# Restaging the mLSTM heads of a two-layer streaming encoder: outputs by token, broadcasts by DMA, tails behind the next head

## The reference, cut to what matters

```python
dlog = b[l] - b[s] + i[s]                      # b: running sum of log forget gates; causal
m_t  = max(a[l], max_s dlog);  a = b + m
w    = exp(dlog - m_t);  w_in = exp(a - m_t)
qk   = (q k^T) * w
num  = qk @ v + w_in * (q @ C)
den  = sum_s qk + w_in * (q @ n)
hc   = num / max(|den|, exp(-m_t))
C    = w_in_last * C + (w_last * k)^T v ;  n = w_in_last * n + (w_last * k)^T 1
out  = sigmoid(o_pre) * head_norm(hc) * gain   # mean and variance over the head's 128 features
y    = concat(gla, out) @ c_w_out
```

## Time and profile before

| | |
|---|---|
| median of 3 runs | 1608.72 us |
| profiled execution, its own time | 1611.44 us |
| its span | 1609.8 us |
| PE, weight loads of PE | 92%, 86% busy |
| VectorE, ScalarE, GpSimd | 45%, 32%, 5% busy |
| mean granted TensorE clock | 0.946 of full |
| chain that ended last | PE 81%, VectorE 8%, ScalarE 4% |

### The profile page before, as it was taken

The page is one execution under the profiler, slowest core; times in us unless marked ns, Lnnn a source line. Parts: engine busy times, 40 slices in busy tenths (PEclk is TensorE's granted clock), DMA queues, the critical chain, the costliest instruction groups (busy, mean ns, idle before and its releaser), DMA issues.

```text
span 1609.8 us, 29103 instructions
## 1 busy us (share of the span) xinstructions
PE 1474.7 (92%) x11188; PEld 1380.6 (86%) x11188; DVE 722.2 (45%) x1167; ACT 522.1 (32%) x792; POOL 85.5 (5%) x99
## 2 busy tenths in 40 slices
PE   5889999989999999999698988888969999999997
PEld 3878888979999999998587867666969999999997
DVE  4664565463333333335734354444563333333344
ACT  4344344242222222223533343332242212222233
POOL 0000000001100110110100000000001100110110
PEclk9899999999999999999797977887989999999999
DMA  9445253763352344223021111110213323323322
GB/s 327 114 146 166 89 161 108 268 244 115 91 183 79 91 142 132 79 70 77 5 77 32 52 36 37 36 36 17 79 54 90 90 81 90 91 81 89 92 66 82
DMA packets 223377, 160.78 MB, mean 100 GB/s; under 512 B 9226, under 2 KB 209628, under 8 KB 223196
## 3 DMA queue, kind: packets, MB, share of 16 engines
q1 hardware_dynamic: 211728, 117.18, 25.0%
q10 hardware_dynamic: 6764, 25.30, 4.2%
q0 software_dynamic: 4832, 17.58, 3.5%
HBM read 156.46 MB, written 3.57 MB: 99 GB/s over the span
## 4 chain that ended last, share of the span: by engine, by line
PE 81%; DVE 8%; ACT 4%; issue 3%; DMA 2%; ACTq 1%; DVEq 0%; SPq 0%
PE ring L535 68%; PE core_j L451 2%; DVE weight_low L413 1%; PE core_j L751 1%; ACT weight_high L408 1%; PE core_k L756 1%; PE core_k L451 1%; PE core_k L1156 1%; DMA weight_raw<-in_a_w_out 1%; PE core_k L1198 1%; DMA mixer_area<-in_w_mod 1%; PE core_k L1115 1%; PE core_k L1118 1%; ACTq L1907 1%; PE ring L1175 0%
## 5 line engine op out<-in xcount | busy, mean ns | idle before, releaser
L535 PE MATMUL ring<-normed_high,weight_high 128*128 128x272 f32 x2128 | 455.9, 296 | 31.1 <-DVE normed_low L633 14.0
L535 PE MATMUL ring<-normed_high,weight_low 128*128 128x272 f32 x2128 | 447.9, 292 | 0.0
L535 PE MATMUL ring<-normed_low,weight_high 128*128 128x272 f32 x2128 | 447.8, 293 | 0.0
L535 PEld LDWEIGHTS ring<-normed_high,weight_high 128*128 128x128 f32 x2128 | 343.0, 193 | 41.9 <-issue 36.5
L535 PEld LDWEIGHTS ring<-normed_low,weight_high 128*128 128x128 f32 x2128 | 343.5, 194 | 0.0
L535 PEld LDWEIGHTS ring<-normed_high,weight_low 128*128 128x128 f32 x2128 | 340.9, 193 | 0.0
L413 DVE TENSOR_TENSOR weight_low<-weight_raw,weight_high 128x1024 fp32r<-128x1024 f32 x197 | 261.1, 1327 | 136.9 <-ACT weight_high L408 134.8
L408 ACT ACTIVATE weight_high<-weight_raw 128x1024 fp32r<-128x1024 f32 x197 | 206.7, 1050 | 168.4 <-PE ring L535 142.1
L535 PE MATMUL ring<-mixed_high,weight_high 128*128 128x272 f32 x960 | 203.1, 293 | 11.5 <-DVE weight_low L413 9.1
L535 PE MATMUL ring<-mixed_high,weight_low 128*128 128x272 f32 x960 | 200.9, 291 | 0.0
L535 PE MATMUL ring<-mixed_low,weight_high 128*128 128x272 f32 x960 | 200.6, 291 | 0.0
(11 more groups left out here) (378 smaller groups left out, 1150.0 us busy)
## 6 DMA issues: line engine op xcount, KB each, us to landing
weight_raw<-in_w_ffn_in SPq DMA_DIRECT2D x88, 512.0 KB, 3.9
mixer_area<-in_w_mod ACTq DMA_DIRECT2D x12, 2048.0 KB, 10.7
mod_weight<-in_w_mod POOLq DMA_DIRECT2D x16, 1024.0 KB, 5.9
weight_raw<-in_w_ffn_out SPq DMA_DIRECT2D x32, 512.0 KB, 3.7
weight_raw<-in_a_w_in SPq DMA_DIRECT2D x24, 512.0 KB, 4.9
weight_raw<-in_c_w_in SPq DMA_DIRECT2D x20, 512.0 KB, 3.9
mixer_area<-in_w_mod SPq DMA_DIRECT2D x7, 1024.0 KB, 13.3
weight_raw<-in_w_ffn_out SPq DMA_DIRECT2D x16, 384.0 KB, 3.3
```

Source lines behind the costliest of these rows:

```text
L535: last = pe.matmul(PS[p.slot][:, half, 0:HALF], w[n.slot][:, k, :], x[:, k, half * HALF:(half + 1) * HALF], start=(k == 0 and w is WH and ...
```

## The change

1. Row broadcasts by DMA. The two spreads of RA and RI go; SyncE issues a DMA that reads one partition's row (544 floats, 2176 bytes) 128 times and writes it to all partitions: `BA[h % 2]` for the decay row, `WB[h % 2]` for w_in. Both are double-buffered. VectorE reads BA from SBUF for the exponents.
2. The spread of exp(-m) goes. It is transposed once, in the GLA stage, into a small tile FLOOR (tokens on partitions, one column for each head).
3. The heads' outputs are made by token: tokens on partitions, 128 features and the denominator as column 129 (VO has one ones column, states are 129 wide): one chain of matmuls in place of two.
4. Statistics by `bn_stats` and `bn_aggr` on VectorE, the reciprocal root by an integer start value and three Newton steps on a tile of 128 x 5; then one pass for each block that subtracts the mean and scales, transposes back by PE (`head_transposes`), gate (`gated_out`), high and low halves with the gain folded in.
5. The order: the heads are written out. The tail of head h-1 stands between the steps of head h on all three engines. The next head's projection is cut in two halves around the update (`project_part`); in the last head its place is taken by parts of the output projection's first two chains (`out_part`). Head 0's o_pre projection stands in the tail of the last GLA head, in halves around the variance. The output projection uses ahead=2.

```diff
-                sp.wait_ge(s_nd, h)
+                sp.wait_ge(s_mkt, h)
                 sp.dma_start(WQK, t["mlstm_w_qk"][0, h]).then_inc(s_mw2, 16)
                 sp.dma_start(WV, t["mlstm_w_v"][0, h]).then_inc(s_mw2, 16)
-                sp.dma_start(SEL[0:HEADS, :], t["selectors"][h]).then_inc(s_mw2, 16)
+                sp.wait_ge(s_rexp, 2)
+                if h >= 2:
+                    sp.wait_ge(s_ex, h - 1)
+                sp.dma_start(BA[h % 2], RA[h:h + 1, :].unsqueeze(1).to_broadcast([1, P, T])).then_inc(s_ba, 16)
+                if h >= 2:
+                    sp.wait_ge(s_cn, h - 1)
+                sp.dma_start(WB[h % 2], RI[h:h + 1, :].unsqueeze(1).to_broadcast([1, P, T])).then_inc(s_bw, 16)
+                sp.wait_ge(s_nd, h)
...
                 head_mean(pe, OT, s_o, 2 * i + HEADS + 1)
+                if i:
+                    item_part(7, range(0, KD // 2))
                 head_var(pe, OSQ, s_osq, 2 * i + HEADS + 1)
+                if i:
+                    item_part(7, range(KD // 2, KD))
...
+                def next_part(first):
+                    if last:
+                        out_part(*((0, 1) if first else (2, 3)))
+                    else:
+                        project_part(pe, Turn(W_ML, 2, 2, h), r(h, 4), range(0, 4) if first else range(4, KD))
...
+                next_part(True)
+                pe.wait_ge(s_kw, h + 1)
+                for b in range(NB + 1):
+                    n = P if b < NB else TS
+                    mm = pe.matmul(J[:, b // 3, (b % 3) * (P + 1):(b % 3 + 1) * (P + 1)], KW[0:n, b, :], VO[0:n, b, :],
+                                   start=True, stop=True)
+                mm.then_inc(s_cu, 1)
+                next_part(False)
                 pe.wait_ge(s_am, h + 1)
-                spread(RF, K).then_inc(s_be, 1)
-                pe.wait_ge(s_kw, h + 1)
-                pe.wait_ge(s_enb, h + 1)
-                for b in range(NB):
-                    pe.matmul(K[:, b // 2, (b % 2) * 256:(b % 2) * 256 + 256], KW[:, b, :], VO[:, b, :],
-                              start=True, stop=True)
-                pe.matmul(J[:, 1, 0:256], KW[0:TS, NB, :], VO[0:TS, NB, :], start=True, stop=True).then_inc(s_cu, 1)
-                if not last:
-                    project(pe, Turn(W_ML, 2, 2, h), r(4))
+                pe.wait_ge(s_qi, h + 1)
                 pe.wait_ge(s_cn, h + 1)
-                pe.wait_ge(s_qi, h + 1)
-                for b in range(NB):
-                    cols = slice(b * P, (b + 1) * P)
-                    for part, dst in ((0, K), (1, J)):
-                        c = slice(part * P, (part + 1) * P)
-                        pe.matmul(dst[:, 0, cols], VO[:, b, c], AM[:, b, :], start=True, stop=(b == 0))
-                        if b:
-                            pe.matmul(dst[:, 0, cols], CN[:, b - 1, c], QI[:, cols], start=False, stop=True)
-                for part, dst in ((0, K[:, 1, P:P + TS]), (1, J[:, 1, 0:TS])):
-                    c = slice(part * P, (part + 1) * P)
-                    pe.matmul(dst, VO[0:TS, NB, c], AM[0:TS, NB, 0:TS], start=True, stop=False)
-                    mm = pe.matmul(dst, CN0[:, c], QI[:, TP:T], start=False, stop=True)
+                for b in range(NB + 1):
+                    n, cols = (P, slice(b * P, (b + 1) * P)) if b < NB else (TS, slice(TP, T))
+                    mm = pe.matmul(by_block(K, b), AM[0:n, b, 0:n], VO[0:n, b, :], start=True, stop=(b == 0))
+                    if b:
+                        mm = pe.matmul(by_block(K, b), QI[:, cols], CN[:, b - 1, :] if b < NB else CN0,
+                                       start=False, stop=True)
                 mm.then_inc(s_nd, 1)
-                pe.wait_ge(s_dabs, h + 1)
-                head_mean(pe, OT, s_o, h + 2 * HEADS)
-                head_var(pe, OSQ, s_osq, h + 2 * HEADS)
-            with pe.Fori(0, HEADS - 1) as h:
-                head(h)
-            head(HEADS - 1, True)
+            out_part(4, 5)
+            head_transposes(HEADS - 1)
+            out_part(6, 7)
...
+            def moments(h):
+                dve.wait_ge(s_nd, h + 1)
+                dve.wait_ge(s_d2, h + 1)
+                for b in range(NB + 1):
+                    n = P if b < NB else TS
+                    st.add(dve.bn_stats(BN6[0:n, b, :], by_block(K, b, P)))
+                st.wait()
+                for b in range(NB + 1):
+                    n = P if b < NB else TS
+                    st.add(dve.bn_aggr(MV[0:n, b, :], BN6[0:n, b, :]))
+                st.done(dve.tensor_tensor(DEN2, DEN2, FLOOR[:, :, h], ALU.max))
+                st.done(dve.tensor_tensor(VAR, MV[:, :, 1], DEN2, ALU.add))
+            def scale(h):
+                rsqrt(dve, st, VAR, RSTD, RTMP)
+                for b in range(NB + 1):
+                    n = P if b < NB else TS
+                    ins = dve.tensor_scalar(ON[0:n, b, :], by_block(K, b, P), MV[0:n, b, 0:1], RSTD[0:n, b:b + 1],
+                                            ALU.subtract, ALU.mult)
+                    if b < NB:
+                        st.add(ins)
+                ins.then_inc(s_on, 1)
+            def gated_out(h):
+                dve.wait_ge(s_otr, h + 1)
+                dve.wait_ge(s_gah, h + KD + HEADS + DONE0)
+                g = TG[h % 2]
+                st.add(dve.scalar_tensor_tensor(out=OB[:, 0:TP], in0=g[:, 0:TP], scalar=1.0, in1=K[:, 0, :],
+                                                op0=ALU.add, op1=ALU.mult))
+                dve.scalar_tensor_tensor(out=OB[:, TP:T], in0=g[:, TP:T], scalar=1.0, in1=K[:, 1, 0:TS],
+                                         op0=ALU.add, op1=ALU.mult).then_inc(s_ob, 1)
+            def low(h):
+                dve.wait_ge(s_ob, h + 2 * HEADS + 1)
+                st.wait()
+                dve.wait_ge(s_gah, h + KD + HEADS + DONE0 + 1)
+                dve.scalar_tensor_tensor(out=GL[:, h + 4, :], in0=OB, scalar=HGAIN[:, h + 8:h + 9],
+                                         in1=GH[:, h + 4, :].bitcast(F32), op0=ALU.mult,
+                                         op1=ALU.subtract).then_inc(s_glo, 1)
...
+                if h:
+                    low(h - 1)
+                if last:
+                    lo_of(dve, w(h, 3))
+                else:
+                    exponents(h + 1)
...
+        def rsqrt(dve, st, v, y, tmp):
+            st.done(dve.tensor_scalar(y.bitcast(I32), v.bitcast(I32), 1, None, ALU.logical_shift_right))
+            st.done(dve.tensor_scalar(y.bitcast(I32), y.bitcast(I32), -1.0, float(0x5f3759df), ALU.mult, ALU.add))
+            for _ in range(3):
+                st.done(dve.tensor_tensor(tmp, y, v, ALU.mult))
+                st.done(dve.scalar_tensor_tensor(out=tmp, in0=tmp, scalar=-0.5, in1=y, op0=ALU.mult, op1=ALU.mult))
+                st.done(dve.scalar_tensor_tensor(out=y, in0=tmp, scalar=1.5, in1=y, op0=ALU.add, op1=ALU.mult))
...
-            out_act(act, W_OUT1, R_OUT1, 3)
-            hi_of(act, Turn(W_FFN1 + 1))
+            out_act(act, W_OUT1, R_OUT1, 3, ahead=2)
```

More of the change, by code:

```diff
@@ L23 @@
 U32 = mybir.dt.uint32
+I32 = mybir.dt.int32
 ACT = mybir.ActivationFunctionType
@@ L516, in project, with project_part @@
             last.then_inc(s_used, 1)
+        def project_part(pe, n, p, ks):
+            if ks[0] == 0:
+                pe.wait_ge(s_lo, n.index + 2)
+                pe.wait_ge(s_free[p.slot], p.before)
+            for k in ks:
+                last = product(pe, n, p, k, KD, (HNH, HNL))
+            if ks[-1] == KD - 1:
+                last.then_inc(s_used, 1)
         def project_two(pe, n, p, normed):
@@ L705, in transpose_blocks, with out_two, out_pe @@
             return pe.transpose(dst_s, src[:, TP:T], IDENT)
[L707 to L713, removed]
-                for j in range(2):
-                    last = product(pe, Turn(w, j), Turn(p, j), k, len(order), (GH, GL))
+        def out_two(pe, w, p, order, s_tiles, tiles, part=None):
+            part = range(len(order)) if part is None else part
+            if part[0] == 0:
+                for j in range(2):
+                    pe.wait_ge(s_lo, w + j + 2)
+                    pe.wait_ge(s_free[Turn(p, j).slot], Turn(p, j).before)
+            for n in part:
+                pe.wait_ge(s_tiles, tiles - (len(order) - 1 - n))
+                for j in range(2):
+                    last = product(pe, Turn(w, j), Turn(p, j), order[n], len(order), (GH, GL))
                     if n == len(order) - 1:
                         last.then_inc(s_used, 1)
-        def out_pe(pe, w, p, kt, s_tiles, tiles, order=None):
-            if order is not None:
+        def out_pe(pe, w, p, kt, s_tiles, tiles, order=None, begun=False):
+            if order is None:
+                pe.wait_ge(s_tiles, tiles - 1)
+            elif not begun:
                 out_two(pe, w, p, order, s_tiles, tiles)
-            else:
-                pe.wait_ge(s_tiles, tiles - 1)
             with pe.Fori(0 if order is None else 1, KD // 2) as i:
```

(31 more changed lines are left out.)

276 lines of the change are left out of this document (139 added, 137 removed).

## The result

The changed kernel took 1583.70 us (median of 4 runs, 1580.66 to 1588.21) beside 1606.57 for the kernel before (1602.82 to 1611.73): ratio 0.985, 95% interval 0.982 to 0.988. That is 22.9 us less (19 to 30 by the interval). Forecast were 1577 us, 32 less, and faster. Its profiled execution took 1588.21 us with a span of 1586.7, which is 23.1 less than before. Some executions fall into a slower state with a lower granted clock; the comparisons leave them out, and with them the trace of the kernel with PE kept busy, which is of that kind.

What follows compares the result with a forecast made beforehand. It took PE as the kernel's bound, but each mLSTM head's dependence chain as what ends last. Entry, three 33.8 us periods and exit ended at 1142.5 against 1174.5, saving 32 us: 1577 us, 8-in-10 range 1538 to 1594.

Steps and rivals of the forecast that it cites:

- Part 3: Row broadcasts by DMA: each lands in 12.6 us because one partition feeds one engine's worth; bounds 2.8 and 17.0.
- Part 4: One head, k by token to the next: 33.8 us, with VectorE waiting for the broadcast and outputs at half clock.
- Part 2: VectorE's work: five bn_stats and five bn_aggr take 1.9 us, bounds 1.0 and 4; 20.6 us a head in all.
- Part 5: Entry and exit around the heads: head 0's k by token ends near 974.5, the last projections at 1142.5 us.
- Last head: scores, half of out parts, update, half, outputs: 10.8: Exit: from the last head's k by token to the end of its outputs, 10.8 us, ending at 1086.7.
- the 2.2 us for a PE that idled again: Last head's tail: 2.2 us of the 13.8 between its outputs and the end of two output projections.
- the sign set for the exit: First two output projections end 13 to 15 us after the last head's outputs; a stall of about 4.4 us follows.
- the queue at the entry: Head 0: u weight of head 1 waits behind two broadcasts; k by token ends near 974.5, without the queue 971.5.
- Costs taken as nothing: FLOOR 0.4 us at most, written-out loops 0 (between -1 and +3), out_two's wait met long before.
- A: Rival: broadcasts land in 2.8 us like weight loads, a head is PE's 23.4 us, 1542 us; chance 0.28, C included.
- B: Rival: queue is the cycle, 8.6 us per microsecond of landing past 13, slower from 16.3; 1615 us, chance 0.07.
- C: Rival: bn_stats at twice a pass, aggregates 0.2; VectorE bounds a head at 24.6 us with quick broadcasts; chance within A's 0.28.

Runs made afterwards that it cites:

- the kernel with PE kept busy: The changed kernel with 56 matmuls nobody reads put into PE's wait ahead of the outputs of heads 0 to 2: 1573.8 us.
- the ladder of sources: The changed kernel with 278.5 KB transfers added behind the last store, read from different partitions or device memory: 11.8 us from one partition, 2.35 from all 128.
- the rows from memory: The changed kernel with the rows b - m and w_in stored once to device memory and broadcast from there: 1546.14 us, ratio 0.960.
- both edits: The changed kernel with both rows broadcast from device memory and the decay row's broadcast issued at the start of a head: 1547.64 us.
- the decay row early: The changed kernel with the next head's decay row broadcast issued at a head's start, behind two weight loads, not after k by token: 1548.47 us, ratio 0.962.

## Why the prediction was right, and where it was off

**The broadcast (Part 3).** Taken 12.6 us, measured 12.4 to 13.3 in the heads and 11.8 by itself. The reason given, one source partition, is shown by the ladder of sources and by the rows from memory.

**The period (Part 4).** Predicted 33.8 us, measured 34.9, 33.4 and 34.5; VectorE's wait 6 to 9 us, measured 10.4, 10.9 and 9.9 (it came to the exponents earlier than I had it); PE's idle time as said, 8.5 at most, and the half clock in the outputs. `v`, taken at 2.2 us, ran at half clock in two of three heads (2.57) and at the full clock in the third (1.43).

**The statistics (Part 2).** Five `bn_stats` took 1.09 us and five `bn_aggr` 0.44: 1.5 where 1.9 was taken. With the two small steps behind them it is 1.8, where Part 5 has 2.3. Both lie within the bounds.

**The sum, term by term**, from the start of the last GLA variance:

| | predicted | measured |
|---|---|---|
| to the end of head 0's k by token | 53.3 | 49.4 |
| three periods | 101.4 | 102.9 |
| last head's k by token to its outputs | 10.8 | 17.8 |
| outputs to the end of the first two output projections | 13.8 | 11.0 |
| stall for the next pair's halves | 4.4 | 4.4 |
| six projections | 37.6 | 38.7 |
| together | 221.3 | 224.2 |

The term that failed is "Last head: scores, half of out parts, update, half, outputs: 10.8". It lists PE's instructions and leaves out what the first needs: the second output weight's low half, which VectorE makes behind weighted keys, attention, q and the tile's low half, and ScalarE's high half before it. With those two moved the stretch was 11.2 us, so the list itself was right within 0.4 and the missing wait cost 6.5 us. The entry was 3.9 us too dear and the tail 2.8, which paid most of it back; that is luck. In the tail the 2.2 us for a PE that idled again were not on the path, since gate and low half stand between the transposes and the last tile, and the sign set for the exit (13 to 15 us) was not met.

A part of the entry's 3.9 is this execution. In it the pairs of L1140 and L1143 ran at 0.22 us, in the changed kernel's traces with sources added behind and with the last halves early mostly at 0.43, and there the entry took 51.9 and 52.0 us, 1.4 under the forecast. Behind these pairs (from the end of L1145 to the end of k by token) all three take 31.5 us; with rows from memory it is 28.4, with both edits 27.1. So the queue at the entry was worth 3.1 to 4.4 us, against the 3.0 of the prediction.

**The time.** The forecast saving of 32 us came out as 29.2 in the stretch and as 22.9 in the medians. 2.8 us of that distance are the terms above. The other 6 were not located. Executions of the same instructions differ by up to 7 us ahead of the heads, which is enough for them, but a cost of the change there isn't ruled out.

**Costs taken as nothing** (FLOOR, written-out loops, `out_two`): the piece where the stretch starts is reached at 922.5 us in the median of twelve traces, between 920.2 and 927.1, and at 921.16 in the one trace before. That agrees with the bounds given, -1 to 3, and cannot tell them from nothing.

**The rivals.** A's condition, a quick landing, was not met here; with another source it is, and its 23.4 us a head came out as 23.0 to 23.2. B's rate was shown with longer transfers, and its threshold (16.3 us of landing) was not reached. C's dearer statistics were not met (1.5 us for the ten), and done twice they cost 0.8 us a head once the landing was out of the way; behind a late landing they were not tried.

## What to carry to other kernels

A DMA's landing depends on where it is read from, not only on its size; one row of SBUF sent to all partitions took five times as long as the same bytes read from all of them, and a copy of the row in device memory, or a request one stage earlier, costs a few lines. When a wait is taken out of a loop, look at the copies of the loop that differ (here the last head): a list of one engine's instructions is not a sum until each has its operand's maker beside it. Count a stall with the clock it leaves behind.

## What the runs showed of the hardware

- Reading 278.5 KB took 11.8 us from one partition, 13.0 from partitions 0 to 3, 7.2 from 0, 32, 64 and 96, 4.6 from 0 to 15, 3.1 from every eighth, 2.35 from all, 3.2 from one row of device memory.
- Two such reads in one queue, from partitions 0 and 64, took 19.9 us together, two from neighbouring ones 22.0, one alone 11.8.
- While such reads are in flight other transfers are late too. The 64 KB store of a head's state, on GpSimd's queue, took 1.8 us and took it again with the rows from memory; in the changed kernel it took 5.7, with the decay row early 4.4. These are lines of the issues of the two kernels, decay row early first:

```profile
out_C_p<-mixer_area POOLq DMA_DIRECT2D x4, 64.0 KB, 4.4
```
```profile
out_C_p<-mixer_area POOLq DMA_DIRECT2D x4, 64.0 KB, 1.8
```

- SyncE itself is held: behind the two broadcasts of head 0 the issue of a 64 KB load took 7.18 us in the changed kernel, and 0.86 at the same place with the rows from memory; the same load's issue in head 1 took 0.33:

```profile
947.22 7.18 SPq L1031 DMA_DIRECT2D mixer_area<-in_state_mlstm_C  x1
```

- PE's clock stayed at the full once PE had no idle stretch (0.97 to 1.00 in the periods of the kernels with early or memory rows), and work that nobody reads held it too: with it at the entry, the granted clock from 955 to 968 us was 1.00 and q and k took 1.13 and 0.94 us.
